# A decoder block on one core: the second norm's mean square summed chunk by chunk beside the output projection, its scale and shift applied by the transposing products

## What is computed

```
mod = jax.nn.silu(c) @ ada_w[l] + ada_b[l]
sh_a, sc_a, g_a, sh_f, sc_f, g_f = [m[:, None, :] for m in jnp.split(mod, 6, axis=-1)]
h = rms_norm(x, attn_pre_g[l]) * (1 + sc_a) + sh_a
y = token_mixer(h, ...)              # ends in  merged @ w_out
x = x + g_a * rms_norm(y, attn_post_g[l])
h = rms_norm(x, ffn_pre_g[l]) * (1 + sc_f) + sh_f
y = peer_ffn(h, ...)                 # begins with  h @ w_q
x = x + g_f * rms_norm(y, ffn_post_g[l])
```

## Time and profile before

| | us |
|---|---|
| median of 3 runs | 2384.16 (2382.42 to 2392.72) |
| the profiled execution, its own time | 2380.1 |
| its span, first to last instruction | 2378.3 |
| PE busy in the span | 1951.4 (82%) |
| DVE busy | 1294.1 (54%) |
| ACT busy | 459.6 (19%) |
| POOL busy | 723.8 (30%) |
| mean granted clock of PE | 0.911 of full speed |
| output projection, first tile to last | about 836 to 932.7 |
| gap, last tile to the first query product | 932.7 to 957.4 |
| query projection | 957.4 to 1048.8 |

### The profile page before, as it was taken

How to read it: one execution, slowest core, us unless ns; L and a number is a source line. 1 busy time by engine, 2 the same in 40 slices (tenths; PEclk the granted TensorE clock), 3 DMA queues, 4 the chain that set the end, 5 groups by cost and what they waited for, 6 DMA issues and landing times.

```text
span 2378.3 us, 17076 instructions
## 1 busy us (share of the span) xinstructions
PE 1951.4 (82%) x5531; PEld 998.2 (42%) x5531; DVE 1294.1 (54%) x2172; ACT 459.6 (19%) x999; POOL 723.8 (30%) x657
## 2 busy tenths in 40 slices
PE   2789999999999986985777788787768878887786
PEld 0335564444456875872333333333323333333332
DVE  6855224664265646545555555555475555555553
ACT  0001012222234434431111111111121111111101
POOL 2112000000000001006543654465345445644560
PEclk9889889999999998997998998989988888988898
DMA  9979536776565564539999999999999999999996
GB/s 348 368 257 340 192 106 213 254 253 226 172 230 183 178 241 140 169 119 421 406 415 421 415 421 420 422 415 415 421 409 412 419 419 423 421 421 421 422 421 262
DMA packets 161460, 774.89 MB, mean 326 GB/s; under 512 B 15024, under 2 KB 21332, under 8 KB 86016
## 3 DMA queue, kind: packets, MB, share of 16 engines
q0 software_dynamic: 91648, 637.57, 66.2%
q1 hardware_dynamic: 67376, 130.69, 16.4%
q10 hardware_dynamic: 2384, 5.95, 0.7%
HBM read 772.03 MB, written 2.13 MB: 326 GB/s over the span
## 4 chain that ended last, share of the span: by engine, by line
PE 41%; DMA 29%; DVE 10%; issue 9%; POOL 9%; ACT 1%; DVEq 0%; POOLq 0%; ACTq 0%
DMA arena<-in_peer_u_dram,idx_now 25%; PE PS L844 14%; PE PS L1215 10%; POOL arena L512 8%; DMA arena<-in_ada_w_dram 3%; PE PS L1193 2%; PE PS L837 2%; PE PS L839 2%; PE PS L838 2%; DVE arena L1275 2%; DVE arena L1329 1%; PE PS L1195 1%; PE PS L1017 1%; DMA arena<-in_cmp_w_dram 1%; PE PS L1003 1%
## 5 line engine op out<-in xcount | busy, mean ns | idle before, releaser
L1215 PE MATMUL PS<-arena 128*128 128x512 f32 x2048 | 1008.6, 656 | 290.2 <-ACT arena L797 272.6
L1684 DVE CUSTOM_DVE_ANT_0 arena<-arena 128x2048 f32<-128x2048 f32 x256 | 586.4, 2292 | 484.4 <-DMA arena<-in_peer_u_dram,idx_now 483.9
L1215 PEld LDWEIGHTS PS<-arena 128*128 128x128 f32 x2048 | 426.4, 211 | 872.3 <-issue 551.5
L844 PE MATMUL PS<-arena 128*128 128x512 f32 (+1 forms) x912 | 407.9, 592 | 0.0
L512 POOL DMA_INDIRECT arena<-in_peer_v_dram,idx_now x256 | 321.1, 1254 | 256.6 <-PE PS L1215 182.4
L512 POOL DMA_INDIRECT arena<-in_peer_u_dram,idx_now x256 | 318.5, 1244 | 104.1 <-issue 83.7
L844 PEld LDWEIGHTS PS<-arena 128*128 128x128 f32 x912 | 168.3, 192 | 175.4 <-issue 168.8
L791 ACT ACTIVATE act_g<-dots 128x4 f32<-128x4 f32 x64 | 13.1, 205 | 940.5 <-DVE dots L1684 940.5
L1532 DVE TENSOR_TENSOR w_lo<-w_raw,w_hi 128x1024 fp32r<-128x1024 f32 x96 | 117.0, 1225 | 137.5 <-ACT w_hi L697 137.2
L450 POOL DMA_DIRECT2D arena<-in_ada_w_dram x64 | 34.0, 531 | 489.4 <-DVE arena L1329 274.6
L1329 DVE SCALAR_TENSOR_TENSOR arena<-arena,csil 128x2048 f32<-128x2048 f32 x60 | 141.1, 2351 | 13.4 <-DMA arena<-in_ada_w_dram 11.9
(11 more groups left out here) (245 smaller groups left out, 1682.9 us busy)
## 6 DMA issues: line engine op xcount, KB each, us to landing
arena<-in_ada_w_dram POOLq DMA_DIRECT2D x96, 1024.0 KB, 5.8
arena<-in_w_in_dram SPq DMA_DIRECT2D x112, 512.0 KB, 5.7
w_raw<-in_w_out_dram SPq DMA_DIRECT2D x32, 512.0 KB, 3.7
w_raw<-in_peer_w_q_dram SPq DMA_DIRECT2D x32, 512.0 KB, 3.6
w_raw<-in_w_branch_nsa_dram SPq DMA_DIRECT2D x16, 512.0 KB, 4.0
w_raw<-in_w_branch_mla_dram SPq DMA_DIRECT2D x16, 512.0 KB, 3.6
arena<-in_cmp_w_dram SPq DMA_DIRECT2D x8, 512.0 KB, 10.5
arena<-mod_rows SPq DMA_DIRECT2D x4, 1024.0 KB, 8.6
```

Source lines behind the costliest of these rows:

```text
L844: ins = nc.tensor.matmul(PS[:, bank + t, 0:cols], lhs[:, kk, t * P:(t + 1) * P], wring[:, m % WSLOTS, k, 0:cols], start=(kk == 0), stop=(k ...
L1215: ins = nc.tensor.matmul(PS[:, bank + k, :], diag[e % 8], Vrow[e % RING][:, k * NC:(k + 1) * NC], start=False, stop=False, skip_group_chec ...
L1684: v.tensor_tensor_reduce(row, row, h2[:, t, :], 1.0, 0.0, ALU.mult, ALU.add, dots[:, e:e + 1]).then_inc(u_free, 1)
```

## The change

It replaces the gap's order of work by four things.

1. The second norm's mean square is no longer taken from x + r y' (y' = gated y, r = inverse root of the first norm), but as mean(x^2) + 2 r mean(x y') + r^2 mean(y'^2). DVE sums x y' per chunk (`cross_junk`, a multiply with a sum) and also forms `ys` = y' times the scale row; ACT squares y' per chunk (two more squares in `y_squares`) and both halves of x (in chunk 1). The product x times the scale row moves to the ends of chunks 1 and 2, both on DVE; POOL's product goes.
2. In the gap h is formed without the second inverse root and without the shift, in eight pieces of 512 channels. The transposition becomes a product with `diag_r`, the identity times the inverse root, and the shift is added by a product of four partitions, started before it in the same bank (`shift_first`, `turn_h2`). The last four pieces are turned between the query projection's tiles Q2 and Q4.
3. The two rows are loaded right after `sk_raw`, together with 8 KB of the shift in another layout, and x is loaded after ACT's `w_high` of tile 7. The experts' gate row moves behind the load of tile Q23.
4. x + r y' itself and the full h, which the experts need, are formed on DVE in chunk 1 of the query projection.

The diff, cut to its core:

```diff
 # sync
                 if n == 0:
                     sp.wait_ge(merged_ready, 4)
                     sp.dma_start(sk_raw, peer_sub_keys.rearrange("l h s n d -> n (l h s) d")).then_inc(sk_in, 16)
-                if n == 1:
+                if n == 0:
                     sp.wait_ge(mod_stored, 16 * 4)
-                    for dst, row in ((shift_f_row, 1), (scale_f_row, 2)):
+                    for dst, row in ((scale_f_row, 2), (shift_f_row, 1)):
                         sp.dma_start(dst, mod_dram[row, :].partition_broadcast(P)).then_inc(rows_f_in, 16)
+                    sp.dma_start(shift_k[0:4, :, :], mod_dram[1, :].rearrange("(a b d) -> b a d", a=4, b=4)).then_inc(shift_in, 16)
...
-                if n == 1:
+                if n == 2:
+                    sp.wait_ge(h2b_ready, 8)
                     sp.dma_start(gate_f_row, mod_dram[3, :].partition_broadcast(P)).then_inc(last_row_in, 16)
 # gpsimd
-            pool.wait_ge(rows_f_in, 32)
-            pool.wait_ge(x1_ready, 1)
-            pool.tensor_tensor(h2[:, 0, :], X[:, 0, :], scale_f_row, ALU.mult).then_inc(h2a_ready, 1)
 # scalar
+                for t, made, done in ((1, y_mul1, y_sq1), (0, y_mul0, y_sq0)):
+                    act.wait_ge(made, n + 1)
+                    act.wait_ge(done, n + 1)
+                    nc.scalar.activation(sq_y[:, t, :], y[:, t, n * NC:(n + 1) * NC], ACT.Square, scale=float(D) ** -0.5,
+                                         accum_out=sums[:, 1, t, n:n + 1]).then_inc(y_gsq, 1)
...
-                    if n == 1 and m == AHEAD:
+                    if n == 0 and m == TR_LAST + 1:
                         act.wait_ge(merged_ready, 4)
                         for t in range(NT):
                             act.dma_start(X[:, t, :], x_v[:, t, :]).then_inc(x2_in, 16)
+                    if n == 1 and m in (5, 8):
+                        t = m // 8
...
+                        nc.scalar.activation(x_junk, X[:, t, :], ACT.Square, scale=float(D) ** -0.5,
+                                             accum_out=stat[:, 0, t:t + 1]).then_inc(x_sq, 1)
 # tensor
+            def shift_first(n):
+                nc.tensor.matmul(PS[:, 4 + n % 4, :].rearrange("p (a b) -> p a b", b=P), shift_k[0:4, n // 2, :],
+                                 ident[0:4, 0:4].unsqueeze(2).to_broadcast([4, 4, P]),
+                                 start=True, stop=False)
+            def turn_h2(n):
+                a, t = 4 * (n // 2), n % 2
+                pe.wait_ge(h2b_ready, n + 1)
                 for k in range(4):
-                    ins = nc.tensor.transpose(PS[:, (n + 4) % 8, k * P:(k + 1) * P], h2[:, t, (a + k) * P:(a + k + 1) * P],
-                                              ident[:, :])
+                    ins = nc.tensor.matmul(PS[:, 4 + n % 4, k * P:(k + 1) * P], h2[:, t, (a + k) * P:(a + k + 1) * P],
+                                           diag_r[:, t, :], start=False, stop=(k == 3))
...
+            for n in range(4):
+                shift_first(n)
+            pe.wait_ge(diag_made, NT)
+            for n in range(4):
+                turn_h2(n)
...
                     if n == 0 and w % 2 == 0:
-                        pe.wait_ge(h2_lo, 4 + w // 2 + 1)
+                        if w in (2, 4):
+                            for k in range(2):
+                                pe.wait_ge(h2_lo, w - 1 + k)
+                                shift_first(w + 2 + k)
+                                turn_h2(w + 2 + k)
+                        pe.wait_ge(h2_lo, w + 2)
 # vector, end of chunk n of the output projection
+                dve.wait_ge(x2_in, 16 * NT)
+                dve.wait_ge(rows_f_in, 32)
+                if n == 2:
+                    dve.wait_ge(sk_tr, 4)
+                if n == 1 or n == 2:
+                    v.tensor_tensor(h2[:, n - 1, :], X[:, n - 1, :], scale_f_row, ALU.mult)
+                for t, made in ((1, y_mul1), (0, y_mul0)):
+                    dve.wait_ge(made, n + 1)
...
+                    ch.did(v.tensor_tensor_reduce(cross_junk[:, t, :], X[:, t, cols], y[:, t, cols], 1.0 / D, 0.0, ALU.mult,
+                                                  ALU.add, sums[:, 2, t, n:n + 1]))
+                    ch.did(v.tensor_tensor(ys[:, t, cols], y[:, t, cols], scale_f_row[:, cols], ALU.mult))
 # vector, the gap
+            v.tensor_scalar(stat[:, 4, :], stat[:, 1, :], EPS, None, ALU.add).then_inc(msq_ready, 1)
+            ch.did(v.tensor_scalar(stat[:, 0, :], stat[:, 0, :], EPS, None, ALU.add))
+            dve.wait_ge(root_ready, 3)
+            link(v.reciprocal(stat[:, 6, :], stat[:, 6, :]))
+            link(v.tensor_tensor(stat[:, 2, :], stat[:, 2, :], stat[:, 6, :], ALU.mult))
+            link(v.scalar_tensor_tensor(out=stat[:, 2, :], in0=stat[:, 3, :], scalar=2.0, in1=stat[:, 2, :],
+                                        op0=ALU.mult, op1=ALU.add))
+            link(v.tensor_tensor(stat[:, 2, :], stat[:, 2, :], stat[:, 6, :], ALU.mult))
+            v.tensor_tensor(stat[:, 5, :], stat[:, 2, :], stat[:, 0, :], ALU.add).then_inc(msq_ready, 1)
+            def h2_part(n):
+                t, cols = n % 2, slice(n // 2 * NC, (n // 2 + 1) * NC)
+                v.scalar_tensor_tensor(out=h2[:, t, cols], in0=ys[:, t, cols], scalar=stat[:, 6, t:t + 1],
+                                       in1=h2[:, t, cols], op0=ALU.mult, op1=ALU.add).then_inc(h2b_ready, 1)
...
 # vector, query projection
+                    if n == 1 and m in (4, 8):
+                        t = m // 8
+                        dve.wait_ge(h2tr_in, 8)
+                        v.scalar_tensor_tensor(out=X[:, t, :], in0=y[:, t, :], scalar=stat[:, 6, t:t + 1],
+                                               in1=X[:, t, :], op0=ALU.mult, op1=ALU.add)
+                        v.scalar_tensor_tensor(out=h2[:, t, :], in0=h2[:, t, :], scalar=stat[:, 7, t:t + 1],
+                                               in1=shift_f_row, op0=ALU.mult, op1=ALU.add).then_inc(h2_ready, 1)
```

147 lines of the change are left out of this document (82 added, 65 removed).

## The result

The changed kernel takes 2398.82 us (median of 11 runs, 2390.53 to 2403.24) where the kernel before takes 2386.38 (11 runs, 2380.49 to 2392.72): ratio 1.0046, 95% interval 1.0032 to 1.0059. It is slower by about 11 us (7.6 to 14.1); the two medians lie 12.4 apart. The forecast was 2388.5 or +4.3 over the kernel before, and the range reached to 2401. Of the 10.3 us between 2388.5 and the measured median, 2.2 belong to the kernel before, whose median was 2384.16 when the forecast was made.

The account below looks back on a forecast made before the run. Bound taken: PE 41%, transfers 29% of the chain; in the attacked 24.8 us gap, DVE's chain. Terms: -11.6 + 3.5 + 0.8 + 5.0 + 1.6 + 3.1 + 1.9 = +4.3, 2384.4 profiled, 2388.5 as median; range 2372 to 2401.

Parts of the forecast that it names:

- (d): Output projection: DVE's bursts at the ends of chunks 1 and 2 stall PE 2.4 and 2.6 us, together +5.0.
- (e): Output projection: PE's slower clock after the stalls before tiles 19 and 27, 0.8 us each, +1.6.
- (f): Output projection loads: new 7.4 us stall before tile 8 plus 2.65 clock, tile 13's 6.85 gone, net +3.1.
- The moved product: Output projection: x times the scale row on DVE takes 2.2 us, with POOL idle, against 6.48 beside POOL's product.
- (g): Query projection: forming x + r y' and the full h on DVE stalls PE 0.9 us twice, +1.9.
- (a): Gap between output and query projections: DVE's shorter chain starts the first query product 11.6 us earlier, PE keeping up.
- (b): Between the first query tiles: four shift products at 0.45 us and sixteen turning products at 0.11 on PE's path, +3.5.
- (c): Restart of the query projection: the first query products may run at a slower clock, +0.8 us.
- The slow product: Rival, output projection: the 6.48 us is DVE's own, both bursts grow by 4.3, +16.6, 2400.8; chance 0.07.
- the loads fit: Rival, output projection: tile 8 arrives on time, -6.85 for +3.1, total -5.6, kernel 2378.5; chance 0.15.
- loads in a row: Rival, output projection: tile 8 waits for both rows and x at measured landing times, +11.4, 2395.6; chance 0.15.
- the gap shrinks less: Rival, gap: tiny steps and hand-overs between DVE, PE and ACT cost double, saving 6 not 11.6, 2394; chance 0.08.

Follow-up runs that it names:

- fourth experiment: The kernel before with POOL's product of x and the scale row moved to DVE: ratio 0.9999.
- first experiment: The changed kernel with its 32 turning products replaced by transpositions and without the eight shift products: ratio 1.0025.
- experiments 6: The changed kernel with DVE's moved operations spread out and loads in pieces of 256 KB, one behind each tile's load, all from SP: ratio 0.9990.
- 7: The changed kernel with 26 products nobody reads in PE's wait before the turning products: 2395.7 us, a single execution.
- 12: The kernel of the eleventh with 25 products nobody reads ahead of the shift products and 10 behind, and the scale products earlier: ratio 0.9971.
- experiments 5: The changed kernel with DVE's operations of the moved sums spread out, 512 columns at a time behind a `w_low`, loads as in the change: ratio 1.0035.
- second experiment: The changed kernel without the eight shift products alone: ratio 1.0036.
- ninth: The kernel before with sub-keys, rows, x and gate row loaded in pieces, its own sums and order kept: ratio 0.9973.
- eleventh: The changed kernel with spread DVE work, loads in pieces, shift products in two halves and 30 products nobody reads ahead of them: ratio 0.9985.
- the tenth: The kernel of the ninth with POOL's product of x and the scale row moved to DVE: ratio 0.9962, 5 runs.
- third experiment: The kernel before with only its loads of the rows and x moved as in the change, no shift_k load: ratio 1.0025.

## Why the prediction was right in part

The forecast's sum was +4.3, the time came out near +11, inside the range but more than twice the forecast. By its own steps:

- **(d), (e), (f) right in their waits, and in their sum partly by luck:** 3.1 + 5.0 + 1.6 = 9.7 for the output projection, measured 9.3. Tile 8 was to land at 863.5 and PE to wait 7.4 us; it landed at 866.76 in a profile that began this stretch 3.6 later, and PE waited 7.00. The stalls before tiles 19 and 27 were 1.94 and 1.95 for my 2.4 and 2.6, and each took the clock for longer than I gave it (the products of the tile at 0.384 instead of 0.227: 1.8 and 1.7 us for my 0.8 each). Behind tile 8 the clock cost 1.5 (seven products in 3.1 us) for my 2.65. So (f) is 2.8 more stall less 1.2 of clock, 1.6 for my 3.1, (d) 3.9 for 5.0 and (e) 3.5 for 1.6: the errors cancel. That tile 8's landing agrees so well is luck too, since SP's 4.17 us on the rows were not in my sum. The later piece of x landed at 866.2 (853.2 and 13.0 us), tile 8 at 866.76. The Trainium skill (DMA: Bandwidth & Descriptors, Queues, rings and completion order) has a transfer signal only behind earlier writes of the same DMA engine, across queues. The two times agree with the order that I drew from it, tile 8 no earlier than x, but they do not prove the rule: x was started after tile 8 (852.84 against 852.59).
- **The moved product:** 2.28 us for my 2.2, and 2.25 in the fourth experiment. The 6.48 was POOL's doing; the rule of the Trainium skill (SBUF — State Buffer, Who interferes with whom) agrees with these numbers, and the rival that rested on its failing is out.
- **(g) mis-sized:** one stall of 1.04 where I had two of 0.9, and the 1.27 us stall of the earlier trace rows, which I let move on with the gate row, did not return: -0.2 for my +1.9.
- **(a) right on DVE, wrong on PE.** DVE needed 6.7 us from gate products to diagonals, 6.9 by my list (935.62 to 942.5). Then I let PE keep up with DVE; its sixteen turning products took 6.15 us, most of them at half clock, where DVE's other three pieces took 2. The price of (b) is in this too: as transpositions they took 2.8 us less (first experiment). Gap -8.7 for -11.6, or for -10.8 with (c), which cost the first query products nothing.
- **(b) is the step that failed.** "Four shift products of 512 (912 such products took 407.9 us, 0.45 each) and sixteen turning products (0.11 each, as the transpositions)". The 912 of the earlier trace rows are instructions, two to a product, and a transposition is one instruction where a turning product is two. Measured: 1.05 and 0.27 each, 4.3 us an interruption, some 8.4 us for the two where (b) had 3.5; the query stretch grew by 8.4 where (b) and (g) had 5.4. The first two experiments, which take just these products away, give back 3.4 and 2.5 us an interruption, and the first 2.8 us of the gap.
- **Chance, not in the sum:** after the same wait of 1.91 us the score products ran at full clock before (7.41 us) and partly at half after (9.04), and the first top 16, which starts behind the first of them, came 0.9 later. Both values occur among the other kernels, 9.04 in four of them; these still reached the copy in 14.9 to 15.2 us.

No rival came true as written. The slow product and "the loads fit" are refuted; "loads in a row" had +11.4, close to the measured 11, but by a tile 8 that lands 4.5 us later than mine, at 868, and a long stall behind it, and tile 8 landed 0.3 us earlier than mine, each counted from the start of the stretch; "the gap shrinks less" had the right sign for another reason than its hand-overs.

## What to carry to other kernels

Price an operation by a row of the same operation and type, and count instructions against operations in the code before dividing a group's time by its count; a transposition is no price for a product. When work is moved into a stage with slack, ask for the longest uninterrupted piece of it, on the engine and in the queue: 4.6 us of DVE work in one piece cost a stall of 1.9 us and the clock behind it each time, in eight pieces 0.5 to 0.8 us and no clock, and 1 MB loads cost a stall of 5.5 to 9.3 us where the same bytes in pieces of 256 KB, spaced between the tiles and on one queue, cost 0.8 to 1.0. Look, too, at what a moved load has to wait for: that last stall is not the bytes but SP's wait for `merged`, which came to stand ahead of a tile. Before a clever rearrangement, repair the plain stall next to it: the loads in pieces alone gave 0.9973.

## What the runs showed of the hardware

- **PE lost its clock while it was never idle.** This happened five times in four kernels, each time 2.2 to 3.6 us after shift products began, whose operands fill 4 of 128 rows: in the gap of experiments 6 (928.20, fall at 930.4), 7 (945.11, 947.9) and 12 (936.01, 939.3), and within an interruption of experiments 5 (970.21, 973.4) and 6 (950.69, 954.3). Experiment 6, PE busy throughout, then the clock:

```profile
929.00:930.00 1.00, 1.00 (x3) 1.00 0.49 133
930.00:931.00 1.00, 1.00 (x3) 0.72 0.96 317
931.00:932.00 1.00, 1.00 (x2) 0.50 0.20 74
```

  It does not follow each time: no interruption of the changed kernel lost the clock, and in its gap the clock held through the same four and fell 5.2 us after they began, in the idle time that followed. Why these products are followed by a fall is not shown.
- **The same short stall may or may not cost the clock.** Stalls of 1.77 to 2.16 us before tile 19 were followed by slow products in all six kernels that had them (means of 0.327 to 0.384 over a tile). Before tile 27 a stall of 2.01 us was not (second experiment, 60 products at 0.229) where one of 1.95 was (0.256). The wait of 2.00 us before tile 6 stands in every kernel: in ten it was followed by slow products (0.381 to 0.384 over the tile), in the sixth, ninth, eleventh and twelfth experiments by full ones (0.238 to 0.243). These four have loads in pieces and a stall before tile 5 as well, but so has the tenth, which lost the clock.
- **SP's own time to start a transfer can be part of a stall:** 4.17 us for the two row loads of 1 MB each behind the sub-keys, 2.71 for the same two in the third experiment and 1.24 where the kernel before starts them, behind tile 15; each piece of 256 KB in the sixth took under 0.5.
